# A gated linear recurrence on one Trainium2 core: levels scaled by products of the forget gates, and in-projection columns in another order

## What is computed

```python
h = x @ w_in                                   # 1024 -> 4096 columns
q, f, i, g = jnp.split(h, [1024, 2048, 3072], axis=-1)
q = jax.nn.silu(q)
fg = lb + (1.0 - lb) * jax.nn.sigmoid(f)       # forget gate
k = 1.0 - fg
logf = jnp.log(fg)
# per head (8 heads, 128 channels each), over time t:
#   S_t = diag(fg_t) S_{t-1} + k_t i_t^T ;  o_t = S_t^T q_t
o = chunk_gated_linear(heads(q), heads(k), heads(i), heads(logf))
o = rms_norm(o, g_norm) * jax.nn.silu(g)
return o.reshape(B, T, D_MODEL) @ w_o
```

## Time and profile before

| | us |
|---|---|
| median of 3 runs | 1030.84 (1029.82 to 1030.96) |
| the profiled execution | 1026.63 |
| its span in the trace | 1024.7 |
| PE busy | 969.1 (95%) |
| PE weight loads busy | 800.9 (78%) |
| DVE busy | 621.8 (61%) |
| ACT busy | 478.3 (47%) |
| POOL busy | 212.3 (21%) |

### The profile page before, as it was taken

One profiled execution on the slowest core, in us unless ns is written; L12 is line 12 of the kernel. 1 busy time (PEld: TensorE's weight loads), 2 busy tenths in 40 slices (PEclk: granted clock), 3 DMA queues, 4 the chain that ended last, 5 costly groups with the idle time before them and its releaser, 6 DMA issues. The chain is left out here.

```text
span 1024.7 us, 11981 instructions
## 1 busy us (share of the span) xinstructions
PE 969.1 (95%) x4754; PEld 800.9 (78%) x4754; DVE 621.8 (61%) x990; ACT 478.3 (47%) x600; POOL 212.3 (21%) x155
## 2 busy tenths in 40 slices
PE   7889999999998999897999999999999999999995
PEld 5667878888887778796788888877887778888883
DVE  4684576464657846978864555576323566666664
ACT  4554435243432565533344343443656455555552
POOL 2162200000002928622100000001164111212120
PEclk9999999999999999978999999998999999999998
DMA  7880365565656652311566556556533355555621
GB/s 279 179 154 2 114 215 189 181 201 171 203 172 216 211 184 83 124 42 33 190 210 204 177 193 192 180 198 220 176 123 123 126 170 179 182 188 174 197 82 42
DMA packets 103511, 165.90 MB, mean 162 GB/s; under 512 B 3931, under 2 KB 72570, under 8 KB 103456
## 3 DMA queue, kind: packets, MB, share of 16 engines
q1 hardware_dynamic: 99968, 152.61, 44.9%
q0 software_dynamic: 3488, 12.53, 5.4%
HBM read 160.93 MB, written 4.19 MB: 161 GB/s over the span
## 5 line engine op out<-in xcount | busy, mean ns | idle before, releaser
L630 DVE TENSOR_TENSOR wlo<-raw,whi 128x2048 fp32r<-128x2048 f32 (+1 forms) x129 | 296.2, 2314 | 73.3 <-ACT whi L621 73.3
L621 ACT ACTIVATE whi<-raw 128x2048 fp32r<-128x2048 f32 (+1 forms) x142 | 267.9, 1906 | 31.5 <-PE PA L1719 24.4
L1717 PE MATMUL PG<-whi,xlo 128*128 128x512 f32 x576 | 230.0, 399 | 4.8 <-DVE wlo L1300 2.9
L1719 PE MATMUL PG<-whi,xhi 128*128 128x512 f32 x576 | 225.9, 392 | 0.0
L1718 PE MATMUL PG<-wlo,xhi 128*128 128x512 f32 x576 | 225.8, 392 | 0.0
L1717 PE MATMUL PA<-whi,xlo 128*128 128x512 f32 (+1 forms) x344 | 141.0, 410 | 14.5 <-DVE xlo L1092 5.5
L1718 PE MATMUL PA<-wlo,xhi 128*128 128x512 f32 (+1 forms) x344 | 135.5, 394 | 0.0
L1719 PE MATMUL PA<-whi,xhi 128*128 128x512 f32 (+1 forms) x344 | 135.4, 394 | 0.0
L1717 PEld LDWEIGHTS PG<-whi,xlo 128*128 128x128 f32 x576 | 109.3, 190 | 27.5 <-DVE wlo L1300 3.3
L1719 PEld LDWEIGHTS PG<-whi,xhi 128*128 128x128 f32 x576 | 109.0, 189 | 23.2
L1718 PEld LDWEIGHTS PG<-wlo,xhi 128*128 128x128 f32 x576 | 109.3, 190 | 21.4
(11 more groups left out here) (257 smaller groups left out, 1166.7 us busy)
## 6 DMA issues: line engine op xcount, KB each, us to landing
raw<-in_ffn_w_gate SPq DMA_DIRECT2D x44, 512.0 KB, 4.0
raw<-in_ffn_w_up SPq DMA_DIRECT2D x44, 512.0 KB, 5.0
raw<-in_ffn_w_down SPq DMA_DIRECT2D x22, 1024.0 KB, 4.9
raw<-in_w_up SPq DMA_DIRECT2D x44, 512.0 KB, 4.8
raw<-in_hgrn_w_in SPq DMA_DIRECT2D x16, 1024.0 KB, 5.3
raw<-in_w_qkv SPq DMA_DIRECT2D x12, 1024.0 KB, 5.2
raw<-in_w_down SPq DMA_DIRECT2D x11, 1024.0 KB, 4.9
raw<-in_att_w_o SPq DMA_DIRECT2D x4, 1024.0 KB, 5.6
```

Source lines behind the costliest of these rows:

```text
L621: nc.scalar.activation(whi[:, g, 0:n_], raw[:, s, 0:n_], ACT.Copy).then_inc(S("w_hi"), 1)
L630: nc.vector.tensor_tensor(wlo[:, s, 0:n_], raw[:, s, 0:n_], whi[:, g, 0:n_].bitcast(F32), ALU.subtract).then_inc(S("w_lo"), 1)
L1717: mm(dst, xl[:, k, rows], whi[:, g, cols], start=first, stop=False)
L1719: return mm(dst, xh[:, k, rows], whi[:, g, cols], start=False, stop=last_)
```

## The change

The logarithm, the cumulated sum and all exponentials go. The gates themselves are transposed (`hf`, four events more, into `fT`). `qd` starts as q times gate. Going from the shortest level up (m = 1, 2, ... 64), PE multiplies `kTh` and the later halves of `qd`; then `decayed(i)` multiplies `qd` in the later half and `kTh` in the earlier half, in place, by the product of the gates of the whole neighbouring block, which `whole(i)` makes from the level below. Each level thus needs the operands of the level before to be rewritten, and these only after PE has read them; that is done in two parts of four heads. Levels m = 1 to 8 are taken by DVE under a mask; levels m = 16, 32, 64 (i = 4, 5, 6) are copied by ACT block by block (`take(i)` of ACT, 4, 2 and 1 copies for each of 4 banks). POOL has no part in the levels any more.

The column groups now come in the order f, f, q, q, i, g, g, i: the raw gates g are made during the levels, into PG and TB, and the second half of the value products i after the first four heads' outputs. The sigmoid of g runs in front of ACT's `take(4)`, and its product with g and the gain on DVE between `decayed(4)` and cross. `hi(U_H + 17)` stands behind `take(4)` on ACT, and `lo(U_H + 17)` ahead of `decayed(4)` on DVE. Out-projection and transposes of the outputs are interleaved, heads 0 to 3 first.

```diff
-LEVELS = (32, 16, 8, 4, 2, 1)
+LEVELS = 7
+MASKED = 4
...
-    for c in (2, 3, 0, 1, 4, 5, 6, 7):
+    for c in (2, 3, 0, 1, 4, 6, 7, 5):
...
-        dl2 = carve(HH, T)
...
-        TURN = {0: 0, 1: 1, 2: 2, 3: 3, 4: 4, "cross": 5, 5: 6, 6: 7}
-        level_buf = lambda l: dls[TURN[l] % 4]
+        qd = carve(HH, T)
+        decay = [fT]
+        for i in range(1, 7):
+            o = T * HH - (T * HH >> (i - 1))
+            decay.append(flat(lf)[:, o:o + (T * HH >> i)].rearrange("p (h t) -> p h t", h=HH))
         aT = carve(3, HH, P)
...
-            def exponents(l):
-                m = ((CHUNK,) + LEVELS)[l]
-                d = level_buf(l)
-                dv = d.rearrange("p h t -> p (h t)").rearrange("p (b s m) -> p b s m", s=2, m=m)
-                bv = bT.rearrange("p h t -> p (h t)").rearrange("p (b s m) -> p b s m", s=2, m=m)
-                nb = bv.shape[1]
-                mid = bv[:, :, 0, m - 1:m].broadcast_to([P, nb, m])
...
-            for l in range(4):
-                exponents(l)
-            pool.wait_ge(S("lv_full"), 4)
-            exponents(4)
...
+            copy_turned("hf", fT, (0, 2))
             hi(U_H + 9)
             full(U_H + 7)
             gate(qh, 1, PG[:, :, :], "q_sig")
-            for j in range(2):
-                act.wait_ge(S("fg"), j + 1)
-                lv = lf[:, :, j * HALF:(j + 1) * HALF]
-                ac.activation(lv, lv, ACT.Ln).then_inc(S("logf"), 1)
+            copy_turned("hf", fT, (4, 6))
             hi(U_H + 10)
+            copy_turned("hk", kTh, (0, 2))
             hi(U_H + 11)
+            copy_turned("hk", kTh, (4, 6))
             full(U_H + 9)
             ac.activation(vi[:, :, 0:HALF], PA[:, 0:2, :], ACT.Copy).then_inc(S("vi"), 1)
-            for b in range(4):
-                act.wait_ge(S("cum"), b + 1)
-                ac.activation(flat(bT[:, 2 * b:2 * b + 2, :]), PA[:, 2 + b % 2, :], ACT.Copy).then_inc(S("bT"), 1)
             hi(U_H + 12)
-            copy_turned("hk", kTh)
             copy_turned("hq", qTh)
-            def level_exp(l):
-                act.wait_ge(S("lv_d"), {"cross": 14, 5: 16, 6: 18}.get(l) or 2 * l + 2)
-                d = flat(level_buf(l))
-                ac.activation(d, d, ACT.Exp).then_inc(S("lv_e"), 1)
-            level_exp(0)
             hi(U_H + 13)
...
+            def take(i):
+                m = 1 << i
+                for b in range(4):
+                    act.wait_ge(S("lv_full"), 4 * i + b + 1)
+                    for o in range(0, P, 2 * m):
+                        src = PA[o:o + m, b, 0:4 * CHUNK].rearrange("p (g c) -> p g c", g=4)[:, :, o // 2:o // 2 + m]
+                        last = ac.activation(aT[o:o + m, 0:2, 2 * b:2 * b + 2, o + m:o + 2 * m]
+                                             , src.rearrange("p (r c) m -> p r c m", r=2), ACT.Copy)
+                    last.then_inc(S("lv_copied"), 1)
+            hi(U_H + 14)
             full(U_H + 11)
+            ac.activation(sg[:, :, 0:HALF], PG[:, :, :], ACT.Copy).then_inc(S("g_raw"), 1)
+            hi(U_H + 15)
+            hi(U_H + 16)
+            full(U_H + 13)
+            ac.activation(sg[:, :, HALF:D], TB[:, :, :], ACT.Copy).then_inc(S("g_raw"), 1)
+            act.wait_ge(S("g_raw"), 2)
+            ac.activation(flat(fT), flat(sg), ACT.Sigmoid).then_inc(S("g_sig"), 1)
+            take(4)
+            hi(U_H + 17)
+            take(5)
+            take(6)
+            def squares_of(b, bank):
+                act.wait_ge(S("ho"), b + 1)
...
+            for b in range(2):
+                squares_of(b, PA[:, b, :])
+            hi(U_H + 18)
+            full(U_H + 15)
             ac.activation(vi[:, :, HALF:D], PG[:, :, :], ACT.Copy).then_inc(S("vi"), 1)
...
+            x_hi("ho", (0,))
+            for b in range(2):
+                squares_of(2 + b, PG[:, b, :])
+            x_hi("ho", (1,))
+            hi(U_HO + 3)
+            x_hi("ho", (2, 3))
...
+            def decayed(i):
+                for part in range(2):
+                    vec.wait_ge(S("lv_full"), 4 * i + 2 * part + 2)
+                    q_, k_ = pairs(qd, i, part)[:, :, 1, :], pairs(kTh, i, part)[:, :, 0, :]
+                    ve_.tensor_tensor(q_, q_, spread(i, 0, part), ALU.mult)
+                    ve_.tensor_tensor(k_, k_, spread(i, 1, part), ALU.mult).then_inc(S("lv_x"), 1)
+            def whole(i):
+                d = flat(decay[i - 1]).rearrange("p (b s) -> p b s", s=2)
+                link(ve_.tensor_tensor(flat(decay[i]), d[:, :, 0], d[:, :, 1], ALU.mult))
...
+            vec.wait_ge(S("hconst"), 1)
             freed(vec, ev["hq"] + 3)
-            vec.wait_ge(S("hconst"), 1)
-            take(7)
-            products(0)
+            for part in range(2):
+                ve_.tensor_tensor(half(qd, part), half(qTh, part), half(fT, part), ALU.mult).then_inc(S("lv_x"), 1)
+            take(MASKED)
             lo(U_H + 13)
-            products(1)
+            whole(1)
+            decayed(0)
             take(0)
+            for i in range(2, 7):
+                whole(i)
             lo(U_H + 14)
-            products(2)
+            decayed(1)
+            take(1)
             lo(U_H + 15)
-            take(1)
+            decayed(2)
             take(2)
             lo(U_H + 16)
-            products(3)
-            products(4)
+            decayed(3)
             take(3)
-            vec.wait_ge(S("lv_e"), TURN["cross"] + 1)
-            dx = level_buf("cross")
-            ve_.tensor_tensor(dx[:, :, 0:P], dx[:, :, 0:P], kTh[:, :, 0:P], ALU.mult).then_inc(S("lv_x"), 1)
-            ve_.tensor_tensor(dx[:, :, P:T], dx[:, :, P:T], qTh[:, :, P:T], ALU.mult).then_inc(S("lv_x"), 1)
-            take(4)
-            products(5)
-            products(6)
-            take(5)
+            lo(U_H + 17)
+            decayed(4)
+            vec.wait_ge(S("g_sig"), 1)
+            link(ve_.tensor_tensor(flat(sg), flat(sg), flat(fT), ALU.mult))
+            decayed(5)
+            gv = flat(sg).rearrange("p (g c) -> p g c", c=DH)
+            link(ve_.tensor_tensor(gv, gv, gno.unsqueeze(1).broadcast_to([P, RT * HH, DH]), ALU.mult))
...
+                ve_.tensor_tensor(q_, q_, decay[6][:, hs, 2:3].broadcast_to([P, 4, CHUNK]), ALU.mult)
+                k_ = kTh[:, hs, 0:CHUNK]
+                ve_.tensor_tensor(k_, k_, decay[6][:, hs, 1:2].broadcast_to([P, 4, CHUNK]), ALU.mult)\
+                   .then_inc(S("lv_x"), 1)
...
+            mean_squares(0)
+            mean_squares(1)
+            gated(0, PA[:, 0, :])
+            gated(1, PA[:, 1, :])
+            x_lo("ho", (0,))
+            lo(U_HO + 2)
+            mean_squares(2)
+            mean_squares(3)
+            x_lo("ho", (1,))
+            gated(2, PG[:, 0, :])
+            gated(3, PG[:, 1, :])
+            lo(U_HO + 3)
+            x_lo("ho", (2, 3))
...
+            up_tiles(U_H + 6, gate_bank, range(4))
+            pe.wait_ge(S("kr"), 1)
+            turn_tiles("hf", lf, (0, 2))
+            up_tiles(U_H + 6, gate_bank, range(4, 8))
+            pe.wait_ge(S("kr"), 2)
+            turn_tiles("hf", lf, (4, 6))
             pe.wait_ge(S("f_sig"), 2)
-            up(U_H + 8, lambda r: PA[:, r, :])
-            pe.wait_ge(S("qh"), 1)
-            pe.wait_ge(S("logf"), 2)
-            pe.wait_ge(S("hconst"), 1)
-            for b in range(4):
-                if b >= 2:
-                    pe.wait_ge(S("bT"), b - 1)
-                for c in range(2):
-                    for r in range(RT):
-                        last = mm(PA[:, 2 + b % 2, (2 * c + r) * P:(2 * c + r + 1) * P],
-                                  lf[:, r, (2 * b + c) * DH:(2 * b + c + 1) * DH], ucum, start=True, stop=True)
-                last.then_inc(S("cum"), 1)
-            pe.wait_ge(S("kr"), 2)
-            turn_rows("hk", kr)
+            up_tiles(U_H + 8, low, range(3))
+            turn_tiles("hk", kr, (0, 2))
+            up_tiles(U_H + 8, low, range(3, 6))
+            turn_tiles("hk", kr, (4, 6))
+            up_tiles(U_H + 8, low, range(6, 8))
             pe.wait_ge(S("qh"), 2)
             turn_rows("hq", qh)
+            up_tiles(U_H + 10, gate_bank, range(2))
...
                 for b in range(4):
-                    pe.wait_ge(S("lv_taken"), 4 * l + b + 1)
+                    pe.wait_ge(S("lv_x"), 2 * i + b // 2 + 1)
+                    if i <= MASKED:
+                        pe.wait_ge(S("lv_taken"), 4 * i + b + 1)
+                    else:
+                        pe.wait_ge(S("lv_copied"), 4 * (i - MASKED - 1) + b + 1)
...
+                            rows = slice(r * P, (r + 1) * P)
+                            late = qd[:, 2 * b + c, rows].rearrange("p (b s m) -> p b s m", s=2, m=1 << i)[:, :, 1, :]
...
+                            last = mm(PA[:, b, o:o + CHUNK], kTh[:, 2 * b + c, rows], late, start=True, stop=True)
                     last.then_inc(S("lv_full"), 1)
...
-            up(U_H + 10, lambda r: PG[:, r, :])
```

(42 more changed lines are left out.)

167 lines of the change are left out of this document (50 added, 117 removed).

## The result

| | kernel before | changed kernel |
|---|---|---|
| median of six runs, us | 1029.76 | 1023.02 |
| lowest and highest | 1029.03 to 1030.96 | 1018.08 to 1025.51 |
| profiled execution, us | 1026.63 | 1018.08 |
| its span, us | 1024.7 | 1016.3 |
| mixer, first product of the fourth column group (U_H + 6) to the transposes behind the out-projection | 355.26 to 498.89: 143.63 | 353.44 to 490.48: 137.04 |

A forecast was written before the change was run, and what follows sets the result against it. PE was taken to bound the kernel. With own work equal, 17.7 us of waits and slow clock became 9.0 of waits plus 5.0 of clock, a 3.7 us gain: 1030.84 - 3.7 = 1027.1 us, range 1023.3 to 1034.0.

The forecast's parts named there:

- Bounds and stretch: Outside its waits the time is PE's; programs differ only from 355.26 to 498.89 us, 143.6 us to account for.
- the price of a transpose event: In PE's mixer work, eight transpose records were taken as one event of about 0.9 us.
- PE's own work: In the mixer, 125.9 us before and after: the cumulated sum goes (3.65), four transpose events come (3.6).
- Levels 1 to 4: PE's k-tiles cover the operand rewriting; operands ready 2.0, 0.9, 1.6 and 0.6 us ahead, so no new wait.
- rival (e): Cover of levels 1 to 4 fails: DVE 10% slower, PE waits about 0.7 us four times; 1030 us, chance 0.06.
- Level 5: PE waits 6.2 us (5.5 to 7.8) ahead of this level for a chain over ACT and DVE.
- the term of the copies: Sixteen small ACT copies of `take(4)` ahead of level 5: 0.15 us each, 2.4 together, bounds 1.8 to 4.0.
- (d): ACT's small copies cost 0.25 to 0.3 us each, level-5 wait 7.8 to 8.6 us; 1029.1 us, chance 0.12.
- The other waits: PE waits 1.7 us at the third `hq` transpose, 0.4 for the second value half, 0.7 at the last transposes.
- The clock: Falls at the level-5 wait, back at or shortly after the end of the following k-tile; 5.0 us lost, bounds 3.9 and 11.
- (b): Clock stays low through level 6, perhaps cross: 1031.9 to 1034.7 us, centre 1033; chance 0.25.
- (c): Clock is back within level 5, some 2 us lost and not 5: 1024.1 us; chance 0.12.

## Why the prediction was off

**Bounds and stretch: right.** The difference lies between the fourth column group and the transposes behind the out-projection, but for the 1.8 us of an earlier low stretch.

**The failed step: the price of a transpose event.** The forecast had "eight transpose records of one event about 0.9". A row of eight records is two events; one has four and costs 0.45. The same reading is in the row of before, x8 in 1.04 us, and I gave it to one event. It entered the sum of before twelve times and the sum of after sixteen times. The four new events cost 1.8 and not 3.6, so PE's own work did not stay the same but fell by 3.65 - 1.8 = 1.85 us. And the twelve events of before were priced 5.4 us too high: own work was 120.5, not 125.9, and so 143.6 - 120.5 = 23.1 us were waits, slow clock and small gaps, not 17.7.

**A second term stood at nothing without a reason: the small gaps** between the starts of unlike groups. They are what is left of the mixer after own work, waits and clock, 1.8 us.

| us | forecast | by the traces |
|---|---|---|
| own work before | 125.9 | 120.5 |
| waits, clock, gaps before | 17.7 | 23.1 |
| own work after | 125.9 | 118.6 |
| waits after (6.2 + 1.7 + 0.4 + 0.7; 7.1 + 2.5 + 0.7 + 1.0) | 9.0 | 11.3 |
| slow clock after | 5.0 | 5.3 |
| the remainder after, small gaps between starts | 0 | 1.8 |
| gain of the mixer | 3.7 | 6.6 |

I subtracted the waits after in full from waits before that were counted 5.4 too low. The trace of before could have told me. Its waits in the mixer (engine, bank and line, who ended them: total, times, longest) are

```profile
PE TB L1685 <- DVE work L1538: 3.1, 2, 2.7
PE PA L2104 <- issue: 2.7, 1, 2.7
PE TB L1685 <- ACT work L698: 2.6, 3, 2.1
PE TB L1685 <- DVE xlo L1077: 1.8, 1, 1.8
PE PA L2134 <- DVE work L1487: 0.8, 1, 0.8
PE PA L2089 <- ACT work L698: 0.7, 1, 0.7
```

together 11.7. The slow clock cost 5.5 in the two levels, 1.2 in the k-tile behind them and 2.3 around the start of the out-projection, 9.0 in all. That is 20.7 already, more than the 17.7 that my sum left for both. It also says what the change gained: the waits as a whole hardly fell, 11.7 to 11.3, since the new one ahead of level 5 took the place of several; the slow clock fell from 9.0 to 5.3, own work by 1.85, and the remainder from 2.4 to 1.8.

The measured gain exceeds the forecast by 1.85 us of own work and by 5.4 - 2.3 - 0.3 - 1.8 = 1.0 us of the rest, 2.9 together.

The price alone does not account for the miss. With 0.45 for an event and all else as it stood, the gain would have been 3.7 + 16 x 0.45 - 0.9 (the `hq` wait, which is longer by it) = 10.0 us, 3.4 too much, though a range moved with it, 1017.0 to 1027.7, would have held the median. The terms that were too small, the gaps and the wait ahead of level 5 above all, had hidden about half of the wrong price, and that was luck. Of the 4.1 us between 1027.1 and the median, the other 1.1 is the start of the sum, 1030.84 from three runs, where six gave 1029.76. The bounds of the unknown costs were all put on the new waits; none was put on the terms that looked known.

**Levels 1 to 4: right.** No wait ahead of them; rival (e) fell.

**Level 5: right in place, releaser and cause, 0.9 us too short.** `take(4)` is sixteen copies in 3.62 us, 0.226 apiece, nearer to my upper bound (0.25) than to the 0.15 that I took. One of them was busy for 0.213 us on average, so the overlap of 0.1 that I subtracted did not happen between them. Without the term of the copies (1.2 us) the 7.09 would be 5.9. So (d) was true of the copies in part, and it did not decide the time. The other waits came out at 2.53, 0.68 and 0.98. The first is longer by the two events of 0.45, not 0.9, that stand ahead of it: the same error again.

**The clock: the size came out, in part by luck; rivals (b) and (c) did not happen in the two traces of this kernel.** Level 5 lasted 442.25 - 435.40 = 6.85 us for 3.49, the k-tile 2.70 for 1.36, level 6 4.05 for 3.49: 3.36 + 1.34 + 0.56 = 5.3 us lost, 5.0 forecast. The page of the Trainium skill that I had set against it, "TensorE: Matmul & The Clock Gate", Part 1, says that activity releases the throttle; level 5, busy for 6.80 of 6.80 us, did not. With the columns put back PE was at 0.50 through two levels and two k-tiles, from 437.0 to 455.8. How near (b) was is shown by that kernel and its twin with the sigmoid moved, where the clock was back before level 6: no rule that I had separates the three, and in runs of the changed kernel without a trace (b) may have happened.

**The profiled pair against the medians.** One execution each would have given 8.5 us, with the 1.8 us of a low stretch ahead of the change counted as gain.

## What to carry to other kernels

Before a term is called known, count how many records one event of it has, in the program and in the row, and give it bounds as well: an own work that is priced too high hides waits of the same size. When a chain over two engines sets a wait, list what stands in their queues between its members and is not needed yet; here one such instruction moved behind the chain was worth twice the change itself. Here a wait ahead of light work cost its length (7.1 us) and nearly as much again in clock (5.3), so such a wait is best taken away whole or filled with work.
